# Placing two dense blocks of an encoder layer elsewhere, and changing the order of small matmuls inside the steps of a chunked recurrence

## The reference, cut to what matters

```python
z = z + mu_prev * (z_prev - z) + mu_next * (z_next - z)
r, k, v, wd, ad, gd = jnp.split(z, _offsets(RW_SPLIT), axis=-1)
w_log = w0 + jnp.einsum('btdr,drc->btdc', jnp.tanh(wd.reshape(B, T, 2, W_RANK)), w_up)
a = jax.nn.sigmoid((a0 + jnp.einsum('btdr,drc->btdc', ad.reshape(B, T, 2, A_RANK), a_up)).astype(f32))
g = jnp.einsum('btr,rc->btc', jax.nn.sigmoid(gd), g_up)
def step(S, inp):
    r_t, w_t, kh_t, ak_t, v_t, kt_t = inp
    sk = jnp.einsum('bhvk,bhk->bhv', S, kh_t)
    S = S * w_t[:, :, None, :] - sk[..., None] * ak_t[:, :, None, :] + v_t[..., None] * kt_t[:, :, None, :]
    return S, jnp.einsum('bhvk,bhk->bhv', S, r_t)
gates = jax.nn.sigmoid(gate_logits.astype(jnp.float32)).astype(x.dtype).reshape(B, T, N_BRANCH, D)
merged = (gates[:, :, 0] * jnp.einsum('btc,cd->btd', o_rw, w_proj_rwkv)
          + gates[:, :, 1] * jnp.einsum('btc,cd->btd', o_att, w_proj_attn))
```

## Time and profile before

| | |
|---|---|
| median of 3 runs | 3561.52 us (3557.09 to 3565.84) |
| profiled execution, whole time | 3566.13 us |
| its span, first to last instruction | 3564.3 us |
| TensorE busy | 3347.8 us, 94% of the span |
| VectorE, ScalarE busy | 1833.8 us (51%), 990.2 us (28%) |
| mean granted TensorE clock | 0.975 of full speed |

### The profile page before, as it was taken

One profiled execution on the slowest core, in us unless ns is written; L12 is line 12 of the kernel. 1 busy time (PEld: TensorE's weight loads), 2 busy tenths in 40 slices (PEclk: granted clock), 3 DMA queues, 4 the chain that ended last, 5 costly groups with the idle time before them and its releaser, 6 DMA issues. The chain is left out here.

```text
span 3564.3 us, 57177 instructions
## 1 busy us (share of the span) xinstructions
PE 3347.8 (94%) x24648; PEld 2149.8 (60%) x24648; DVE 1833.8 (51%) x3086; ACT 990.2 (28%) x1570; POOL 2.5 (0%) x13
## 2 busy tenths in 40 slices
PE   9999997999999599889999899999899999999997
PEld 4565554454555355568888745556666666666665
DVE  2347762476776478035555423126564454654546
ACT  2334431333433223223333345000321111122121
POOL 0000000000000000000000000000000000000000
PEclk9999999999999799999999999999999999999999
DMA  3210000253453422253443232111112121122211
GB/s 130 67 28 16 15 20 32 72 175 114 136 183 101 164 82 98 106 182 119 131 141 120 99 132 83 67 62 71 47 60 77 60 83 53 60 77 89 83 59 60
DMA packets 199146, 316.53 MB, mean 89 GB/s; under 512 B 50672, under 2 KB 156144, under 8 KB 193776
## 3 DMA queue, kind: packets, MB, share of 16 engines
q1 hardware_dynamic: 198896, 312.87, 25.5%
HBM read 211.26 MB, written 95.03 MB: 86 GB/s over the span
## 5 line engine op out<-in xcount | busy, mean ns | idle before, releaser
L629 PE MATMUL ra_ps<-xT,ra_w 128*128 128x512 f32 (+1 forms) x1152 | 432.0, 528 | 18.8 <-DMA ra_w<-in_w_in 18.0
L629 PEld LDWEIGHTS ra_ps<-xT,ra_w 128*128 128x128 f32 x1152 | 215.1, 191 | 219.4 <-issue 191.4
L1656 PE MATMUL tl_ps<-merged,tl_sums 128*128 128x320 f32 x1088 | 322.3, 436 | 15.3 <-DVE oR L1849 7.8
L997 PE MATMUL rg_ps<-xT,rg_w 128*128 128x512 f32 (+1 forms) x768 | 287.3, 530 | 17.2 <-DMA rg_w<-in_w_gate 17.2
L1849 DVE TENSOR_TENSOR oR<-tl_ps,oR 128x320 f32<-128x320 f32 x416 | 201.9, 489 | 151.6 <-PE tl_ps L1656 149.4
L1656 PE MATMUL tl_ps<-merged,tl_wt 128*128 128x320 f32 x896 | 270.5, 437 | 8.9 <-DMA tl_wt<-in_w_out 8.9
L1656 PEld LDWEIGHTS tl_ps<-merged,tl_sums 128*128 128x128 f32 x1088 | 206.3, 191 | 109.5 <-issue 28.1
L1656 PE MATMUL tl_ps<-tl_Th,tl_sums 128*128 128x320 f32 x864 | 241.2, 436 | 8.4 <-issue 6.1
L997 PEld LDWEIGHTS rg_ps<-xT,rg_w 128*128 128x128 f32 x768 | 145.6, 193 | 138.5 <-issue 115.2
L1656 PEld LDWEIGHTS tl_ps<-merged,tl_wt 128*128 128x128 f32 x896 | 171.9, 192 | 81.4 <-DMA tl_wt<-in_w_out 9.3
L1656 PEld LDWEIGHTS tl_ps<-tl_Th,tl_sums 128*128 128x128 f32 x864 | 165.5, 192 | 78.5 <-issue 11.1
(11 more groups left out here) (236 smaller groups left out, 4710.1 us busy)
## 6 DMA issues: line engine op xcount, KB each, us to landing
rc_ub<-ub SPq DMA_DIRECT2D x80, 640.0 KB, 5.2
ub<-ra_ub SPq DMA_DIRECT2D x32, 1280.0 KB, 5.3
tl_wt<-in_w_ff SPq DMA_DIRECT2D x32, 1024.0 KB, 4.7
tl_wt<-in_w_ff SPq DMA_DIRECT2D x64, 512.0 KB, 3.2
ra_w<-in_w_in SPq DMA_DIRECT2D x24, 512.0 KB, 3.3
ub<-ra_v SPq DMA_DIRECT2D x16, 640.0 KB, 6.1
gates<-rg_gate SPq DMA_DIRECT2D x16, 640.0 KB, 3.7
mg_gate<-gates SPq DMA_DIRECT2D x16, 640.0 KB, 3.9
```

What stands on the lines that cost most here:

```text
L629: last = pe.matmul(ps[:, bank + j, 0:n], w[c][:, 128 * i:128 * i + 128], xT[:, i, t0:t0 + n], start=(i == 0), stop=(i == KT - 1))
L997: last = pe.matmul(ps[:, 3 * (b % 2) + j, 0:n], w[b % 3][:, 128 * i:128 * i + 128], xT[:, i, t0:t0 + n], start=(i == 0), stop=(i == KT - 1))
L1656: last = pe.matmul(bank(n, b), lhs(k), rhs(k), start=(fresh and k == 0), stop=(k == d - 1), skip_group_check=True)
```

## The change

Three parts. First, there is no low-rank stage any more: the blocks wd and ad are made at the head of the scaled stage (function `whole`), and gd is the first block of the gate stage. Second, the first two of the 16 gate blocks are made at the end of the scaled stage, and `lower` of the last pair stands behind the first and the second of them; the gate stage has 15 blocks, with its transposes one to two places earlier in `SLOTS`, and the last inverses are sent after its last block. Third, in the state stage: the values of the next step alternate, `u` by `u`, with the products of KH with the state at the head of a step; the output's state part alternates with the score product onto BB; the corner products go over `u` in the order 0, 4, 1, 5, 2, 6, 3, 7, so that forward and backward ones alternate. ScalarE's `evict` of the next step's values moves ahead of the copy of Bs.

```diff
-def low_rank_stage(nc, hbm, xT, glob, low):
...
@@ scaled_stage, SP @@
+            for c in range(2):
+                sp.dma_start(w[c][:, :], hbm["w_in"][B_LOW + c]).then_inc(w_ready[c], 16)
             sp.dma_start(pcs[:, :, 0:NPAIR], hbm["pcols"]).then_inc(pc_ready, 16)
...
+            for c in range(2):
+                sp.wait_ge(lz_ready, c + 1)
+                weights(c, 0)
             for p in range(PAIRS + 1):
+                if p == PAIRS:
+                    for c in range(2):
+                        sp.wait_ge(z_p[c], PAIRS)
+                        sp.dma_start(w[c][:, :], hbm["w_gate"][c]).then_inc(w_ready[c], 16)
...
+            for c in range(2):
+                sp.wait_ge(gate_done, c + 1)
+                sp.dma_start(hbm["gates"][c], (tq, rs)[c][:, :]).then_inc(gate_sent, 16)
+            sp.wait_ge(gate_sent, 32)
@@ scaled_stage, tensor @@
+            for c in range(2):
+                pe.wait_ge(w_ready[c], 16)
+                whole(c, 3 * c).then_inc(lz_ready, 1)
+            pe.wait_ge(l_mixed, 1)
             for p in range(PAIRS):
...
-            pe.wait_ge(bonus_done, PAIRS)
-            lower(PAIRS - 1, 0, 3)
+            pe.wait_ge(w_ready[0], 16 * PAIRS + 32)
+            pe.wait_ge(mix_s[2], PAIRS)
+            pe.wait_ge(mix_p[2], PAIRS)
+            whole(0, 0).then_inc(gate_ready, 1)
             pe.wait_ge(free6, used(6, PAIRS, "w0"))
             pe.wait_ge(free7, used(7, PAIRS, "w0"))
+            lower(PAIRS - 1, 0, 6)
+            pe.wait_ge(w_ready[1], 16 * PAIRS + 32)
+            pe.wait_ge(bonus_done, PAIRS)
+            whole(1, 3).then_inc(gate_ready, 1)
+            pe.wait_ge(l0_copied, PAIRS)
             lower(PAIRS - 1, 1, 6)
@@ gate_stage @@
+        NB = 2 * KT - 1
...
+            return hbm["w_in"][B_LOW + 2] if b == 0 else hbm["w_gate"][b + 1]
...
-        for b, first, n in ((0, 0, 4), (1, 4, 4), (2, 23, 2)):
+        for b, first, n in ((0, 0, 4), (1, 4, 4), (2, 22, 2)):
...
-        for b, first, n in ((0, 15, 8), (1, 26, 8), (2, 37, 8)):
+        for b, first, n in ((0, 14, 8), (1, 25, 8), (2, 35, 8)):
...
+                            act.activation(gate[0][:, :], set_of(ps, 0), ACT.Copy, scale=glob[:, G_OM + 2:G_OM + 3]).then_inc(l_own, 1)
+                            act.wait_ge(l_mixed, 1)
+                            act.activation(gate[0][:, :], gate[0][:, :], ACT.Sigmoid).then_inc(gate_done, 1)
@@ state_stage, tensor @@
+                if g + 1 < NSTEP:
+                    pe.wait_ge(ub_ready[(g + 1) % 3], 32 * ((g + 1) // 3) + 32)
...
                 pe.wait_ge(s_done, 2 * g + 2)
-                heads(ps, BB, lambda u, h: x[half(h), u, 3 * CH:4 * CH], lambda u, h: S[half(h), u, :], True).then_inc(bd_ready, 1)
-                if g:
-                    pe.wait_ge(o_done, 2 * g)
-                heads(ps, OB, lambda u, h: S[half(h), u, :], lambda u, h: x[half(h), u, 4 * CH:5 * CH], True)
+                for u in range(U):
+                    for h in range(2):
+                        last = pe.matmul(ps[half(h), BB, CH * u:CH * u + CH], x[half(h), u, 3 * CH:4 * CH], S[half(h), u, :],
+                                         start=u == 0, stop=True, skip_group_check=True)
+                    if u == U - 1:
+                        last.then_inc(bd_ready, 1)
+                    if g + 1 < NSTEP:
+                        values(g + 1, u)
...
-                for u in range(U):
+                for u in ALTERNATE:
...
-                heads(ps, BB, lambda u, h: sc[other(h), u, h, 0:CH], lambda u, h: v[other(h), u, h, :], False).then_inc(b_ready, 1)
+                if g:
+                    pe.wait_ge(o_done, 2 * g)
+                for u in range(U):
+                    for h in range(2):
+                        pe.matmul(ps[half(h), OB, CH * u:CH * u + CH], S[half(h), u, :], x[half(h), u, 4 * CH:5 * CH],
+                                  start=u == 0, stop=True, skip_group_check=True)
+                    for h in range(2):
+                        last = pe.matmul(ps[half(h), BB, CH * u:CH * u + CH], sc[other(h), u, h, 0:CH], v[other(h), u, h, :],
+                                         start=False, stop=True, skip_group_check=True)
+                last.then_inc(b_ready, 1)
...
+                    pe.wait_ge(v_done, 2 * g + 4)
                 pe.wait_ge(b_done, g + 1)
...
-                    values(g + 1)
@@ state_stage, scalar @@
                 act.activation(Wt[:, :, :], ps[:, CB, 0:256].rearrange("p (u n) -> p u n", n=32), ACT.Copy, scale=-1.0).then_inc(w_done, 1)
+                if g + 1 < NSTEP:
+                    act.wait_ge(v_ready, g + 2)
+                    if g:
+                        act.wait_ge(o_ready, g)
+                    evict(g + 1)
                 act.wait_ge(b_ready, g + 1)
```

More of the change, by code:

```diff
@@ L625, in _, with whole @@
         def _(pe):
+            def whole(c, bank):
+                for j, (t0, n) in enumerate(SPANS):
+                    for i in range(KT):
+                        last = pe.matmul(ps[:, bank + j, 0:n], w[c][:, 128 * i:128 * i + 128], xT[:, i, t0:t0 + n],
+                                         start=(i == 0), stop=(i == KT - 1))
+                return last
             def span(c, bank, j):
@@ L637, in low_piece @@
                 after(pe, free7, used(7, p, "wa"[which] + str(j)))
+                if p == 0 and j == 0:
+                    pe.wait_ge((l_tanh, l_mixed)[which], 1 + which)
                 for d in range(2):
@@ L744, in lower_out @@
                     act.sem_inc(free6, 1)
+            for c in range(2):
+                act.wait_ge(lz_ready, c + 1)
+                act.activation(low[c][:, :], set_of(ps, 3 * c), ACT.Copy, scale=glob[:, G_OM + c:G_OM + c + 1]).then_inc(l_own, 1)
+                if c == 0:
+                    act.wait_ge(l_mixed, 1)
+                    act.activation(low[0][:, :], low[0][:, :], ACT.Tanh).then_inc(l_tanh, 1)
             act.wait_ge(om_ready, 1)
@@ L804, in _ @@
             dve.wait_ge(set_up, 5)
+            for c in range(2):
+                dve.wait_ge(l_own, c + 1)
+                shift_mix(dve, ch, low[c], set_of(ps, 3 * c), glob[:, G_MP + c:G_MP + c + 1], glob[:, G_MN + c:G_MN + c + 1])
+                dve.sem_inc(l_mixed, 1)
             def mix(p, c, x, parts):
@@ L896, in pv_at, with gate_stage @@
     return 160 * d + NCH * p + c
-def gate_stage(nc, hbm, xT, cst):
+def gate_stage(nc, hbm, xT, cst, glob):
     with Stage(nc, "rg") as st:
@@ L990, in _ @@
             at = 0
-            for b in range(2 * KT):
+            for b in range(NB):
                 pe.wait_ge(w_ready[b % 3], 16 * (b // 3) + 16)
@@ L1163, in scores, with values @@
                 last.then_inc(sc_ready, 1)
-            def values(g):
-                if g:
-                    pe.wait_ge(u_done, 2 * g)
-                for u in range(U):
-                    for h in range(2):
-                        out = 64 * (1 - h)
-                        last = pe.matmul(ps[out:out + 64, UB, CH * u:CH * u + CH], ub[g % 3][64 * h:64 * h + 64, u, 0:CH],
-                                         centre[64 * h:64 * h + 64], start=True, stop=True)
-                last.then_inc(v_ready, 1)
+            def values(g, u):
+                for h in range(2):
+                    last = pe.matmul(ps[other(h), UB, CH * u:CH * u + CH], ub[g % 3][half(h), u, 0:CH], centre[half(h)],
+                                     start=True, stop=True)
+                if u == U - 1:
+                    last.then_inc(v_ready, 1)
             def heads(out, bank, lhsT, rhs, start, skip=True):
```

119 lines of the change are left out of this document (50 added, 69 removed).

## The result

The changed kernel takes 3505.68 us (median of 4 runs, 3503.85 to 3508.09) against 3559.73 us for the kernel before (4 runs beside it, 3557.09 to 3565.84): a ratio of 0.9847, 95% interval 0.9833 to 0.9862. That is 54 us faster where 102 were forecast. It lies in the wide range (3430 to 3518), beside the rival "supply of instructions takes over" (3500). The likeliest case (3460, its own range 3435 to 3485) did not come.

A forecast was written before the change was run, and what follows sets the result against it. TensorE, busy 94% of the span, was taken as the bound, a state step being the sum of its sets. Terms -23 - 80 - 10 + 1 + 10 = -102 gave 3464 us profiled, 3460 median; 8-in-10 range 3430 to 3518.

The forecast's parts named there:

- supply of instructions takes over: Rival, state stage: instruction fetch becomes the bound and takes half of the 90 us gain; about 3500 us, chance 0.21.
- The likeliest case: Four-way work in the state stage with mild instruction supply cost; 3460 us, chance 0.60.
- Seams: Blocks moved between stages: head, tail and gate stage together save 23 us.
- The head: Low-rank and scaled stages: gates fall together and K's first block follows at about 596 us; -37.4 us.
- The tail: Last sums to gate stage, now with two gate blocks: 70.2 us for what took 44.9, +25.
- The gate stage: 15 blocks for 16 (-17.2), less later transposes (+1) and inverses sent last (+5): -11 us.
- The four-way sets and the corners: State stage: two interleaved sets of 64 records take 1.08 us each, -80 us; corners 0.40 a set, -10 us.
- no four-way work: Rival, state stage: interleaved sets still run at 34 ns a record in steady state; 3535 us, chance 0.12.
- a floor per record: Rival, state stage: records start no sooner than 25 ns apart, saving 40 us for 80; 3500 us, chance 0.04.
- slower: Rival, state stage: each quadrant-pair change inside a set costs time; 3598 us at 50 ns a change, chance 0.03.
- Slack: State stage step: the new state is ready 0.3 us before TensorE reaches KH, so no wait there.
- Instruction supply: State stage: idle at borders of 256-instruction packets grows from 0.5 to 0.75 us a step, +10 us.

The follow-up runs named there:

- e1: The changed kernel with the state stage of the kernel before, so only the blocks moved between stages remain; 3533.12 us, ratio 0.9901.
- e3: The changed kernel without the operand loads of state steps 3 to 39 (old operands, state's factors zero); 3479.04 us, ratio 0.9753.
- e8: The kernel of e7 without the operand loads of steps 3 to 39, as in e3; 3458.61 us, ratio 0.9699.
- e7: The changed kernel with the next step's first scores moved into the middle of the dense stretch, same instructions; 3508.75 us, ratio 0.9839.
- e11: The changed kernel with e7's order and each step's operand load cut into eight 160 KB transfers at eight places; 3474.32 us, ratio 0.9748.
- e10: The kernel of e1 with 64 already satisfied waits a step ahead of the scores' matmuls, 32 becoming instructions; 3557.12 us, ratio 0.9983.

## Why the prediction was right and wrong

**Seams: right in place and size.** The head was forecast at -37.4; the last sums end at 1129.59 (1127.28 + 2.31) where they ended at 1164.40, -34.8. The tail was forecast at 70.2 us; from 1129.59 to 1198.10 it takes 68.5, with a first wait of 9.09 for the 7 taken and a first block of 20.53 for 20.5. The gate stage was forecast at -11 and is 324.6 us (1198.10 to 1522.68) against 336.9, -12.3. All together -23.5 for -23 in this execution and -30.6 in e1's, so the level was met within what one execution tells.

**The four-way sets and the corners: right.** 1.09 us for 1.08, twice a step. Corners 0.38 for 0.40. The step of 9.43 us does come, and from 11.75 us (the commonest step before) that is 2.32 x 39 = 90 us less work, as in the terms -80 and -10. The rivals "no four-way work", "a floor per record" and "slower" are out. The records start 17 ns apart over four quadrants. The floor of about 25 ns from start to start that the Trainium skill states ("TensorE: Matmul & The Clock Gate", Wait — 56ns, not 53.3ns?) doesn't hold for them.

**Slack: right.** No step waits at KH for the state.

**"Instruction supply": the term that was too small.** It was taken at 0.75 us a step for 0.5 before, +10 us. Measured: a step of 9.43 us lasts 11.31, that is 1.88 us, and 11.75 lasted 12.25. So the term is (1.88 - 0.50) x 39 = +54 us. 90 - 54 = 36 us is what the stage gave: from its first matmul to that of the merge stage it took 510.2 us (1546.19 to 2056.39) and takes 474.6 (1522.68 to 1997.29). Of the 54, 45 are counted in waits at the borders; the rest is not assigned, a part of it the 14 us more at the lower clock: a set of 32 records (`Bs,NF`) took 1.90 us in such a stretch (1712.28 to 1714.18) and 1.11 outside (1549.74 to 1550.85).
The mechanism was in the prediction and was its first rival; its size was scaled with the mean demand, one packet in 3.7 us for one in 4.9. But time at a border is not lost on the mean. It is lost where 256 instructions are used up faster than the next packet comes. The dense stretch was 384 instructions in 2.95 us, which is 2.0 us for 256, against a spacing of 3.1 to 3.5 us even on idle queues (e3, e8). In the kernel before the densest stretch was 320 instructions in 4.65 us with 0.39 of it idle (1589.65 to 1594.30), 3.4 us for 256: it just met the spacing, so the limit hardly showed (2.9 us of waits that were not for held-back packets). That division was open to the prediction and was not made; the spacing to hold it against came only with the runs. With the loads the packets come later still: 20 us of waits went with the loads (e3), and without the loads spreading took another 24 (e8).
That the total lies in the wide range is the rival's doing: the sum was 48 us off (102 for 54), and the case that came had been given 0.21. Its price, half of the 90 us or 45, came near the measured 54.
The Trainium skill ("Runtime: NRT & Kernel Launch", Instruction fetch mechanics) describes a fetch in blocks of 16 KiB, which the packets here agree with (0.13 MB in 8), and calls the cost of crossing one mostly hidden. The traces disagree for this kernel: 47 of 99 borders cost 1.3 us each.

**Open.** Spreading gave nothing beside the big loads (e7: 66 waits for 47, each shorter, the same 62 us) because TensorE then ran into 19 held-back packets where it had run into 7; why in this order their delays fall where the packet is needed was not taken apart. Nor was it tried whether it is the size or the places of the eight transfers that four did not have: four also ended the long delays, and yet gained nothing.

## What to carry to other kernels

When small matmuls are made to run beside each other, work out how long the densest 256 instructions take, weight loads included, not only the mean of a step: once that falls under the spacing at which packets arrive (some 3.3 us here), further gains are in good part paid back at the borders. "Issue" waits at ever different lines but always at the same remainder of the instruction number are the sign, and the times of the packets on the instruction queue are the proof. Against it help slow, instruction-poor work laid between the dense sets, and bulk loads cut into short transfers spread over the step; each alone gave nothing to 16 us here, both together 31.

## What the runs showed of the hardware that was not expected

- The packet of 256 instructions that TensorE needs next starts only when it has entered the block ahead, 1.1 to 1.2 us behind that border in the median (e3, the changed kernel), moves for 0.9 to 1.5 us, and gives its first instruction at least 1.15 us after its end (14 kernels). Intervals of 256 that TensorE waited for lasted 3.1 to 3.4 us (quartiles) with the DMA share at 0.09 (e3), 3.5 to 4.4 in the changed kernel.
- The operand loads hardly stretch the packet's own transfer (0.96 us in the median in the changed kernel, 1.12 in e3 without them, 1.97 the longest of e11); they delay its start, to as much as 5.81 us behind the border in the changed kernel and 3.41 in e3.
- Two 640 KB loads in one go (5.2 us to landing) cost more than their bytes: eight of 160 KB at eight places, the same bytes, gave 16 us.
- A satisfied wait that is an instruction of its own costs TensorE's queue some 24 ns (e10: 0.77 us for 32 a step), as much as one and a half of the interleaved records.
- With TensorE waiting at the borders for 14% of its steps' time (62.2 of 441 us), the granted clock fell to 0.5 in five stretches of 3.4 to 6.8 us (20.5 us in the changed kernel's steps); in e11's steps it never did. The two don't go strictly together: e7 had the same 62 us of waits and 10.2 us at the lower clock.
